# Squares of the first down-projection's tiles, moved between GpSimd's operator products

## The reference, cut to what matters

```python
def conv_ffn(h, w_up, conv_w, conv_b, w_down):
    a = causal_dwconv(h @ w_up, conv_w, conv_b)
    gate, val = jnp.split(a, 2, axis=-1)
    return (jax.nn.silu(gate) * val) @ w_down

h = h + conv_ffn(rmsnorm(h, norm_ffn[0]), ...)    # layer 0
u = rmsnorm(h, norm_mix[1])                       # layer 1: needs the mean of h*h over all 2048 channels
h = h + s5_mixer(u, ...)                          # x_t = lam_bar * x_(t-1) + b_bar u_t;  y_t = Re(c x_t) + d u_t
```

## Time and profile before

| | |
|---|---|
| Median of three runs | 2409.65 us (2408.2 to 2409.75) |
| The profiled execution's own time | 2408.9 us |
| Its span in the profile | 2407.2 us |
| First down loop and the formed operators | about 1007 to 1336 us |
| Squares, norm and gathering behind it, until L1545 starts | to 1380.65 us |

### The profile page before, as it was taken

The page is one execution under the profiler, slowest core; times in us unless marked ns, Lnnn a source line. Parts: engine busy times, 40 slices in busy tenths (PEclk is TensorE's granted clock), DMA queues, the critical chain, the costliest instruction groups (busy, mean ns, idle before and its releaser), DMA issues.

```text
span 2407.2 us, 40988 instructions
## 1 busy us (share of the span) xinstructions
PE 2196.9 (91%) x12698; PEld 1902.1 (79%) x12698; DVE 1775.1 (74%) x2944; ACT 999.0 (41%) x1425; POOL 465.8 (19%) x464
## 2 busy tenths in 40 slices
PE   5999998979999999889888288697999999999997
PEld 5888875868888888778777188686888888888886
DVE  5677646678888888699999365577888888875555
ACT  4444343334444444333333122354444444444442
POOL 7902000520000000055555400052000000001221
PEclk8999997989999999999999655598999999999999
DMA  4454432545555555466666874554555565556664
GB/s 150 157 175 156 141 123 70 183 131 186 188 184 186 187 184 186 148 180 211 211 213 203 177 201 112 162 175 136 178 191 185 182 191 186 181 186 193 188 189 133
DMA packets 179182, 415.28 MB, mean 173 GB/s; under 512 B 16816, under 2 KB 84528, under 8 KB 179136
## 3 DMA queue, kind: packets, MB, share of 16 engines
q1 hardware_dynamic: 157888, 395.96, 53.1%
q10 hardware_dynamic: 21248, 18.75, 2.4%
HBM read 389.60 MB, written 25.03 MB: 172 GB/s over the span
## 4 chain that ended last, share of the span: by engine, by line
PE 74%; POOL 8%; issue 7%; DVE 6%; DMA 2%; SPq 1%; ACT 1%; DVEq 0%; POOLq 0%; ACTq 0%
PE bank L303 42%; PE bank L302 22%; POOL pq_pt L620 5%; PE bank L299 3%; POOL pt L624 3%; PE bank L1580 2%; PE bank L300 1%; PE bank L1489 1%; DVE ut L353 1%; PE bank L1545 1%; PE bank L1404 1%; DVE lo L283 0%; SPq L449 0%; DMA p_op<-s_pt 0%; POOL ssq L327 0%
## 5 line engine op out<-in xcount | busy, mean ns | idle before, releaser
L303 PE MATMUL bank<-xx,hi 128*128 128x512 f32 x3780 | 1358.0, 401 | 0.0
L302 PE MATMUL bank<-xx,lo 128*128 128x256 f32 x3780 | 1068.6, 283 | 6.7 <-DVE xx L1296 6.7
L283 DVE TENSOR_TENSOR lo<-raw,hi 128x1024 fp32r<-128x1024 f32 x698 | 901.3, 1327 | 89.5 <-ACT hi L276 86.4
L276 ACT ACTIVATE hi<-raw 128x1024 fp32r<-128x1024 f32 x698 | 711.1, 1053 | 382.1 <-PE bank L303 272.6
L303 PEld LDWEIGHTS bank<-xx,hi 128*128 128x128 f32 x3780 | 717.1, 190 | 166.4
L302 PEld LDWEIGHTS bank<-xx,lo 128*128 128x128 f32 x3780 | 721.6, 191 | 17.6 <-issue 7.2
L303 PE MATMUL bank<-aa,hi 128*128 128x512 f32 x1344 | 478.2, 397 | 0.0
L302 PE MATMUL bank<-aa,lo 128*128 128x256 f32 x1344 | 385.7, 287 | 39.6 <-DVE lo L283 39.6
L303 PEld LDWEIGHTS bank<-aa,hi 128*128 128x128 f32 x1344 | 257.3, 191 | 53.3
L302 PEld LDWEIGHTS bank<-aa,lo 128*128 128x128 f32 x1344 | 258.9, 193 | 47.2 <-DVE lo L283 45.6
L954 DVE SCALAR_TENSOR_TENSOR cgv<-sumt,par,cgv 128x255 f32<-128x255 f32 x368 | 179.7, 488 | 54.4 <-DVE cgv L954 26.1
(11 more groups left out here) (246 smaller groups left out, 1732.1 us busy)
## 6 DMA issues: line engine op xcount, KB each, us to landing
raw<-in_up SPq DMA_DIRECT2D x344, 512.0 KB, 3.6
raw<-in_down SPq DMA_DIRECT2D x160, 448.0 KB, 3.9
raw<-in_w_in SPq DMA_DIRECT2D x98, 512.0 KB, 4.0
raw<-in_w_out SPq DMA_DIRECT2D x32, 512.0 KB, 3.6
raw<-in_down SPq DMA_DIRECT2D x32, 512.0 KB, 3.7
raw<-in_glu SPq DMA_DIRECT2D x32, 512.0 KB, 4.0
s_c<-cp ACTq DMA_DIRECT2D x16, 512.0 KB, 6.9
s_pt<-ut ACTq DMA_DIRECT2D x16, 512.0 KB, 2.7
```

Source lines behind the costliest of these rows:

```text
L276: A.activation(hi[:, s, :], raw[:, s, :], ACT.Copy).then_inc(hi_done, 1)
L283: V.tensor_tensor(lo[:, s, :], raw[:, s, :], hi[:, s, :].bitcast(f32), SUB).then_inc(lo_done, 1)
L302: TE.matmul(bank[:, L:], lo[:, s, w], x2[:, k, 0, :], start=False, stop=False)
L303: last = TE.matmul(bank[:, :], hi[:, s, w], x2[:, k, :, :], start=False, stop=k == total - 1)
```

## The change

The squares of tile `t` are computed inside the down loop, behind the products for tile `t + 1`, not behind the loop. `ssq` starts from zeros, so that each tile has the same two operations. The last tile's pair stands behind the loop. The pair in the loop is `tile_squares`, with an index held in a register.

```diff
-            with chain.loop(0, KT // 2, 6) as i:
+            def tile_squares(i, s):
+
+                kt = 2 * i + s
+                g.wait_ge(tile_read, Q_DN0 + 1 + kt)
+                chain(G.tensor_tensor(sqt[:, :], h[:, bass.ds(kt, 1), :].squeeze(1),
+                                      h[:, bass.ds(kt, 1), :].squeeze(1), MUL))
+                chain(G.tensor_tensor(ssq[:, :], ssq[:, :], sqt[:, :], ADD))
+            chain(G.memset(ssq[:, :], 0.0))
+            input_powers(0, 0)
+            input_powers(0, 1)
+            tile_squares(0, 0)
+            with chain.loop(1, KT // 2, 10) as i:
                 input_powers(i, 0)
+                tile_squares(i - 1, 1)
                 input_powers(i, 1)
-            pool_squares(g, chain, 3, Q_DN0)
+                tile_squares(i, 0)
+            g.wait_ge(tile_read, Q_DN0 + KT)
+            chain(G.tensor_tensor(sqt[:, :], h[:, KT - 1, :], h[:, KT - 1, :], MUL))
+            G.tensor_tensor(ssq[:, :], ssq[:, :], sqt[:, :], ADD).then_inc(ssq_ready, 1)
+            g.wait_ge(ssq_ready, 2)
```

## The result

The changed kernel takes 2418.26 us (median of 6 runs, 2416.93 to 2419.41), the kernel before 2409.19 (6 runs). The ratio is 1.0042, with a 95% interval of 1.0032 to 1.0052: 9.1 us slower, where 9.4 were forecast. One run, of experiment 8's second kernel, had a granted TensorE clock of 0.809 where all others have 0.92 to 0.94, took 2515.53 us, and is left out of its median.

What follows compares the result with a forecast made beforehand. VectorE was taken to bound the first down loop at 19.65 us a tile. Loop +11.8, tile 15 -0.4 and tail -2.0 us gave +9.4 us, forecasting 2419.0 us, range 2411.5 to 2424.0.

Steps and rivals of the forecast that it cites:

- The bound: First down loop: VectorE, busy 38.48 of 39.30 us in two tiles, sets 19.65 us a tile; GpSimd idles 8.49 us.
- The price of a pair: In the loop, a tile's two square operations cost VectorE 2 x 0.42 = 0.84 us; 14 pairs, +11.8 us (5.9 to 13.7).
- The place: Behind a tile's last pt operation: the pair starts during VectorE's second split and slows the products after it.
- Tile 15: Last loop tile: two instructions slowed instead of three, so L1167 and the store of s_c come earlier; -0.4 us.
- The tail: Behind the loop: squares end 17 us earlier, but SyncE's load issuing holds the u store; -2.0 us, 0 to 4 allowed.
- Sum: Whole kernel: +11.8 - 0.4 - 2.0 = +9.4 us, forecasting 2419.0 us.
- the 79% for slower: Whole kernel: chance of slowing by over 4.8 us, needing over 0.51 us a pair; main case but its low end, plus GpSimd's full-hold rival.
- my case: Whole kernel: 0.42 to 0.98 us a pair and 0 to 4 us for the tail, 2411.2 to 2423.0 us; 72%.
- the 3% for faster: Whole kernel: chance of over 4.8 us faster, needing the gap-served pair and early-free SyncE rivals together.
- A whole-operation hold: Rival, in the loop: GpSimd holds VectorE for its whole operations, 1.33 us a pair; +16.7 us, 2426.4 us; 7%.
- The pair served in gaps: Rival, in the loop: pair runs in VectorE's short gaps, which loses nothing; -2.4 us, 2407.2 us; 8%.
- SyncE's issuing freed early: Rival, behind the loop: t_op issue time is queue waiting, so the tail gives up to 14.2 us; -2.8, 2406.9 us; 3%.

Runs made afterwards that it cites:

- experiment 8's second kernel: Kernel before with squares on ScalarE, summed by TensorE, and SyncE's first t_op loads in eights in its queue's idle times; 2399.45 us, ratio 0.9965.
- Experiments 1: Kernel before with the squares' pairs added in the down loop, the squares behind the loop kept; 2423.62 us, ratio 1.0062.
- experiment 2: Changed kernel without the pairs in the loop, only the last tile's pair left behind it; 2403.78 us, ratio 0.9982.
- experiment 8: Kernel before with squares on ScalarE, summed by TensorE, in four SyncE load orders; 2404.87, 2399.45, 2402.13 and 2404.66 us.
- Experiment 4: Changed kernel without the add of each loop pair, the multiply alone left; 2410.22 us, ratio 1.0014.
- experiment 3: Changed kernel with the loop's pairs replaced by a one-column product and two write-only memsets; 2405.27 us, ratio 0.9989.
- experiment 5: Changed kernel with each loop pair held back until VectorE's sixth split of the tile, to meet the residual adds; 2413.24 us, ratio 1.0021.
- 8's first: Kernel before with squares on ScalarE, summed by TensorE with ones, SyncE's order unchanged; 2404.87 us, ratio 0.9988.
- experiments 1 and 6: Of these, 6: changed kernel with the 32 first t_op loads moved behind the p_op loads, so u is stored earlier; 2423.27 us, ratio 1.0059.
- experiment 7: First t_op loads issued in eights in SyncE's idle times: on the changed kernel 2412.85 us, ratio 1.0021; on the kernel before 2417.14 us, ratio 1.0041.
- the three last kernels of experiment 8: ScalarE/TensorE squares with t_op loads in eights, 2399.45 us; with the whole gathering ahead of the second eight, 2402.13; without t_op loads between p_op's, 2404.66.

## Why the prediction was right, point by point

- **The bound.** VectorE sets the tile. Experiments 1, 2 and 8 show it: squares on GpSimd lengthen the tile with nothing else changed, squares on ScalarE and TensorE don't.
- **The price of a pair.** The mechanism was right and the size low: 0.84 was taken, 0.944 measured, 13.2 us for 11.8. Rows 5 and 6 gave 0.42 us for each operation as a mean of four, three multiplies and one add. Experiment 4 shows two prices, 0.41 for the multiply and 0.53 for the add. In the old tile 15 the add met L1167, which starts 0.78 us behind the second L1163 where the two L1163 are 0.67 apart: 0.11 us of the add lay in that gap, and the reading from start to start hid it. The steady pair's add meets the second L1163, which waits for nothing. The other price on record, 0.98 us for a pair beside three splits, was nearer to 0.944, and the prediction took it for the upper end only.
- **The place.** As forecast: the splits are unaffected (4.12 us), the two products behind them pay.
- **Tile 15.** -0.4 taken, -0.27 measured.
- **The tail.** -2.0 taken; -2.29 to the store, of which 0.29 is faster issuing (15.48 for 15.77 us). Another 1.11 us up to the first `xs` make 3.40, inside the 0 to 4 us that were allowed for; with the 1.44 us up to the scan it is 4.84, outside of them. The 1.11 us fit both halves of `u` going at once. From the store to the first `xs` pass 19.30 to 19.79 us in the six kernels that issue both halves together ahead of the gathering, with the loads in one block before them (the changed one and experiments 2 to 5 and 8's first), and 20.27 to 20.43 where the halves lie apart (the kernel before, experiments 1 and 6). No run changes this alone. The 1.44 us have no known cause: that stretch takes 26.95 to 29.62 us in eight kernels with SyncE's old order.
- **Sum.** The three errors cancel: +1.4 in the loop, +0.1 in tile 15, about -2.8 behind. The result is nearer to the forecast than its terms are, and that is luck.
- **The chances.** They were added up loosely: the 79% for slower take in all of my case, whose low end they except, and the 3% for faster stand for two rivals of 8% and 3% that must hold together.
- **The rivals.** A whole-operation hold (1.33 us a pair) is refuted by 0.944. The pair served in gaps is refuted by the tile. SyncE's issuing freed early is refuted by 15.48 us for the 32 loads in the changed kernel and 15.55 in experiment 2.

A sentence of the Trainium skill (SBUF — State Buffer, "Who interferes with whom") says that VectorE with two SBUF inputs contends with a GpSimd instruction that reads SBUF and not with one that only writes it. The traces agree: 1.16 and 1.28 us against 0.74 beside the memsets of experiment 3, and an unaffected residual add (one input in PSUM) in experiment 5. The copy that paid in experiment 5 has one SBUF input, and that sentence doesn't cover it.

## What to carry to other kernels

An engine with idle time isn't free if its operations hold back those of the engine that sets the loop: read the bound engine's instructions beside a working and an idle neighbour before moving work under them, and price the move by start-to-start times. Moving work off a tail is worth only the distance to the next thing late, and here that was the program order of a DMA queue, which no busy share shows. Work that suits several engines goes to the one with slack that shares nothing with the bound one.

## What the runs showed of the hardware

- A GpSimd tensor operation of 128 x 256 that reads SBUF delays a VectorE product with two SBUF inputs behind it by its own time less 0.2 us (0.61 to 0.41, 0.72 to 0.53 by difference). Two memsets in its place delay nothing.
- A VectorE copy with one SBUF input also pays: 0.78 us for 0.23 in experiment 5. A residual add from PSUM doesn't. This I had not expected, and the reason is open: no run changed the copy.
- 32 loads of 64 KB in one block took SyncE 15.4 to 16.2 us to issue, 0.48 to 0.51 us each. From the first `xs` to the scan, a stretch in which TensorE waits several times for `p_op` loads, pass 26.95 to 29.62 us in the nine kernels that issue no `t_op` loads between the gathering and the first of these `p_op` loads, and 30.47 to 35.29 in the five that do (experiment 7 and the three last kernels of experiment 8).
- The toll was already there before the change. In the kernel before, GpSimd's operator products fill 1140.79 to 1151.92 almost without a gap, and beside them VectorE's first products of a tile stand longer than the same shapes later on, 3.41 us for two and 1.53 where rows 4 have 0.74, 0.75 and 0.76. That is some 2.8 us a tile, about three times the pair's price. No run moved these products to another engine.

```profile
1143.79 3.41 DVE L1163 TENSOR_TENSOR pq_cp<-bc_in,pw 128x576 f32<-128x576 f32 x2
1147.23 1.53 DVE L1167 TENSOR_TENSOR cp<-pq_cp 128x576 f32<-128x576 f32 x1
```
